# Swapping the two loop levels of the vector engine's gate multiply in a product-key expert layer

## The chip, the cores and the metric

The kernel runs on one core of a Trainium2 chip. The metric is the device time of one execution in microseconds, as the median over executions of the same program. Lower is better.

## The reference

Two transformer blocks are computed in fp32 on 256 tokens of width 1024. The part around the change is the expert layer of the first block: 16384 experts, each a row of `u` and a row of `v`, of which every token takes 16 for each of 8 heads.

```python
q = (xt @ w_q).reshape(BLOCK, PEER_HEADS, PEER_QDIM)
...
t1, i1 = lax.top_k(s1, PEER_TOPK)
t2, i2 = lax.top_k(s2, PEER_TOPK)
...
g = jax.nn.softmax(ts, axis=-1)
act = jax.nn.gelu(jnp.einsum('chkd,cd->chk', u[idx], xt))
coef = (g * act.astype(jnp.float32)).astype(xt.dtype)
return jnp.einsum('chk,chkd->cd', coef, v[idx])
```

## The kernel before

Every weight of the program comes as one stream of 128x128 fp32 tiles, eight to a slab (666 slabs). ScalarE copies each slab to a rounded part `whi` (L390), and VectorE or GpSimd subtracts that from the raw slab to make the remainder `wlo` (L407, in `split_lo`); in the expert layer every third slab goes to GpSimd. TensorE does three matmuls for each tile (`mm3`): high by high, high by low and low by high. The slab loads are issued on the SP queue, which waits for the remainder of the slab three places back.

The expert layer doesn't gather rows. It computes the products of all 128 groups of 128 experts with all tokens (the `u` phase, loop over `e`), applies gelu, and keeps the result in SBUF as two buffers, `act1` and `act2`, each of 64 key indices `i` by 256 tokens `t`, with the token index running fastest: the element (i, t) of a half lies at column 256 i + t. The gate of each (expert, token) pair is zero nearly everywhere. It is built by a product of one-hot matrices: for each group `g` of 8 tokens, VectorE writes the one-hot matrix `ohA` of the second key (L1838), the one-hot matrix `oh` of the first key (L1840) and its product with the three bf16 parts of the gate, `ohB` (L1845). TensorE then runs 24 matmuls of 64 columns into one PSUM bank (8 tokens by 64 key indices, the key index running fastest), and `multiply` (L1847 to L1851) multiplies the piece of the `act` buffer that belongs to these 8 tokens by that bank, in place. In half 0 the profile calls the one-hot buffers `act` too, because they lie in `act2`, which is free until then; in half 1 they have buffers of their own, `ohA`, `oh` and `ohB`.

There are 32 groups in each half. The steps are spread by hand over the tile stream: `coef_tiles` puts the 34 steps of half 0 among the `u` tiles of `e` from 64 to 111, and the 34 steps of half 1 among the `v` tiles of `e` from 0 to 60. A step `j` on VectorE is `multiply(half, j - 2)` and then `onehots(half, j)`. On TensorE, the step for group `g` waits for the multiply of group g - 4 (its PSUM bank is one of four) and for `ohB` of group `g`. In the `v` phase each finished chunk `act[e]` (256 contiguous columns) is split again, by ScalarE into `c` high (`c_hi`) and by VectorE into `c` low (L330), and then multiplied with the `v` tiles. All instructions of an engine run in the order in which the program gives them, so that the multiply stands in VectorE's queue among the slab remainders, the one-hot operations and the `c` remainders.

Of the kernel before, what the change touches and what calls it, by code (L numbers as in the profile page):

```python
# [15 lines left out]
ALU = mybir.AluOpType  # L16
# [9 lines left out]
NX = 256  # L26
# [37 lines left out]
TG, NCF = 8, 3  # L64
# [1599 lines left out]
def dve_peer(k, ring):  # L1664
    V, s, b, p, PS, vec = k.V, k.s, k.b, k.p, k.PS, k.nc.vector
# [179 lines left out]
        s["oh"].inc(vec.tensor_tensor(out, one, rows, ALU.mult))  # L1845

    def multiply(half, g):  # L1847
        v = p.halves[half][:, :].rearrange("p (i t) -> p i t", t=NX)[:, :, TG * g:TG * g + TG]
        V.wait_ge(s["cpe"], NG * half + g + 1)
        V.wait_ge(s["gelu"], HK * (half + 1))  # L1850
        s["coef"].inc(vec.tensor_tensor(v, PS[:, 4 + g % 4, :].rearrange("p (t i) -> p i t", t=TG), v, ALU.mult))  # L1851

    def coefs(half, j):
        if j > 1:
            multiply(half, j - 2)
        if j <= NG:
            onehots(half, j)
# [1345 lines left out]
```

## Time and profile before

| | |
|---|---|
| median of three executions | 2210.39 us |
| lowest and highest | 2207.11 and 2212.05 us |
| the profiled execution | 2212.05 us, its span 2210.7 us |
| TensorE busy in the span | 97% |
| VectorE busy in the span | 73% |
| ScalarE, GpSimd busy | 52%, 29% |
| mean granted TensorE clock | 0.992 |
| the 64 multiplies at L1851 | 43.7 us in all, starting from 557.4 to 955.6 us |

The span runs from the first to the last instruction; 1.35 us of the profiled execution's time lie outside it. Busy times of TensorE are of pipelined matmuls whose ends are modelled, so whether TensorE is held up is read from its waits and from the distance between the starts of its instructions.

### The profile page before, as it was taken

The numbers are of one execution on the slowest core, as the hardware profiler recorded it, in microseconds if no ns is written. First come the engines' busy times: TensorE is split into PE (matmuls) and PEld (weight loads), VectorE is DVE, ScalarE is ACT, GpSimd is POOL, SyncE is SP. The second block draws the span as 40 slices with busy tenths as digits, with TensorE's granted clock in tenths as the row PEclk, the third lists the DMA queues.
The fourth block names the chain that finished last, engine by engine and source line by source line (L and its number), as shares of the span: only waits on it lengthen the run. The fifth ranks groups of instructions, "written<-read, shape, count | busy, mean of one in ns | idle before, by whom it ended". The sixth has DMA issues, their size and how long they took to land.

```text
span 2210.7 us, 44628 instructions
## 1 busy us (share of the span) xinstructions
PE 2150.5 (97%) x18600; PEld 2113.3 (96%) x18600; DVE 1621.7 (73%) x2601; ACT 1160.2 (52%) x1980; POOL 630.7 (29%) x510
## 2 busy tenths in 40 slices
PE   8999999999999999999999999989999999999997
PEld 8898999999999999999999998979999999899997
DVE  7787767798987499965567647988655864788664
ACT  6776565454333444444465445756455544566443
POOL 7422244233222232333333004963001100113001
PEclk9999999999999999999999999999999999999999
DMA  5432455555445544455555554215554655544553
GB/s 169 156 129 96 156 167 177 177 184 175 163 153 159 177 155 162 159 177 182 184 171 188 184 191 134 68 48 162 191 191 141 195 188 193 177 139 152 192 192 114
DMA packets 101143, 357.35 MB, mean 162 GB/s; under 512 B 12048, under 2 KB 15440, under 8 KB 100816
## 3 DMA queue, kind: packets, MB, share of 16 engines
q1 hardware_dynamic: 100080, 352.35, 48.7%
q8 instruction: 148, 2.42, 0.4%
q10 hardware_dynamic: 864, 2.16, 0.3%
q14 instruction: 51, 0.42, 0.1%
HBM read 352.86 MB, written 1.05 MB: 160 GB/s over the span
## 4 chain that ended last, share of the span: by engine, by line
PE 82%; DVE 9%; POOL 3%; ACT 3%; issue 2%; DMA 1%; SPq 0%; POOLq 0%; ACTq 0%; DVEq 0%
PE PS L319 82%; POOL dgl L2975 2%; DVE wlo L407 2%; DVE H L2649 1%; DVE bn L2600 1%; DVE w L2714 1%; DMA raw<-stream 1%; DVE H L2647 1%; ACT whi L327 1%; DVE XC L1056 1%; ACT bsq L327 0%; DVE n L330 0%; DVE gate L1232 0%; POOL XC L1302 0%; DVE XR L1171 0%
## 5 line engine op out<-in xcount | busy, mean ns | idle before, releaser
L407 DVE TENSOR_TENSOR wlo<-raw,whi 128x1024 fp32r<-128x1024 f32 x546 | 686.6, 1260 | 216.5 <-ACT whi L327 215.7
L327 ACT ACTIVATE whi<-raw 128x1024 fp32r<-128x1024 f32 (+1 forms) x667 | 698.9, 1050 | 165.5 <-PE PS L319 101.5
L319 PE MATMUL PS<-bn,whi 128*128 128x256 f32 x3328 | 595.5, 281 | 16.4 <-ACT bn L327 4.9
L319 PEld LDWEIGHTS PS<-bn,whi 128*128 128x128 f32 x3328 | 509.8, 188 | 22.2 <-issue 12.0
L407 POOL TENSOR_TENSOR wlo<-raw,whi 128x1024 fp32r<-128x1024 f32 x119 | 324.2, 2725 | 695.5 <-ACT whi L327 695.4
L319 PE MATMUL PS<-n,whi 128*128 128x256 f32 (+1 forms) x2784 | 516.7, 287 | 5.3 <-DVE wlo L404 3.3
L319 PE MATMUL PS<-bn,wlo 128*128 128x256 f32 x1664 | 459.1, 280 | 0.0
L319 PEld LDWEIGHTS PS<-n,whi 128*128 128x128 f32 x2784 | 436.1, 192 | 9.5 <-issue 4.0
L319 PE MATMUL PS<-n,wlo 128*128 128x256 f32 (+1 forms) x1392 | 395.6, 284 | 0.0
L319 PE MATMUL PS<-c,whi 128*128 128x256 f32 x2048 | 372.3, 284 | 0.0
L319 PEld LDWEIGHTS PS<-c,whi 128*128 128x128 f32 x2048 | 318.9, 192 | 0.0
L319 PEld LDWEIGHTS PS<-bn,wlo 128*128 128x128 f32 x1664 | 313.0, 188 | 0.0
L319 PE MATMUL PS<-c,wlo 128*128 128x256 f32 x1024 | 289.5, 283 | 0.0
L319 PEld LDWEIGHTS PS<-n,wlo 128*128 128x128 f32 x1392 | 267.7, 192 | 0.0
L319 PE MATMUL PS<-hh,whi 128*128 128x256 f32 x1408 | 253.6, 283 | 0.0
L319 PEld LDWEIGHTS PS<-hh,whi 128*128 128x128 f32 x1408 | 219.6, 192 | 0.0
L319 PE MATMUL PS<-hh,wlo 128*128 128x256 f32 x704 | 199.2, 283 | 0.0
L319 PEld LDWEIGHTS PS<-c,wlo 128*128 128x128 f32 x1024 | 196.3, 192 | 0.0
L330 DVE TENSOR_TENSOR c<-act,c 128x256 fp32r<-128x256 f32 x128 | 81.2, 635 | 113.4 <-ACT c L327 113.4
L327 ACT ACTIVATE c<-act 128x256 fp32r<-128x256 f32 x128 | 53.5, 418 | 207.2 <-PE PS L319 207.2
L327 ACT ACTIVATE act<-PS 128x256 f32<-128x256 f32 x128 | 49.3, 385 | 210.6 <-PE PS L319 210.5
L1943 POOL TENSOR_TENSOR acc<-bsq 128x256 f32<-128x256 f32 x12 | 11.1, 922 | 468.5 <-ACT bsq L327 468.5
(351 smaller groups left out, 2995.1 us busy)
## 6 DMA issues: line engine op xcount, KB each, us to landing
raw<-stream SPq DMA_DIRECT2D x666, 512.0 KB, 3.3
abias<-c_alibi ACTq DMA_DIRECT2D x1, 1536.0 KB, 6.3
H<-xt SPq DMA_DIRECT2D x4, 256.0 KB, 6.2
out<-H SPq DMA_DIRECT2D x3, 256.0 KB, 2.4
mask<-c_mask SPq DMA_DIRECT2D x1, 272.0 KB, 6.5
K<-Vh SPq DMA_DIRECT2D x2, 136.0 KB, 4.6
K<-Vl SPq DMA_DIRECT2D x2, 136.0 KB, 5.1
out<-H ACTq DMA_DIRECT2D x2, 128.0 KB, 1.9
```

The source lines that it names most:

```text
L319: return self.nc.tensor.matmul(out, l, r, start=start, stop=stop, skip_group_check=True)
L327: return self.nc.scalar.activation(out, in_, func, **kw)
L330: return self.nc.vector.tensor_tensor(out, x, hi.bitcast(F32), ALU.subtract)
L407: k.s[q].inc(me.e.tensor_tensor(lo[:, :], raw[:, :], hi[:, :].bitcast(F32), ALU.subtract))
L1056: ins = vec.scalar_tensor_tensor(b.XC[:, m, :], b.XR[:, m, t:t + T], col("cw", t * NC + m), b.XC[:, m, :], ALU.mult, ALU.add)
L1943: s["acc"].inc(pool.tensor_tensor(k.acc, sq[:, 0, :] if c == 1 else k.acc, sq[:, c, :], ALU.add))
L2600: s["pre_lo"].inc(k.nc.vector.scalar_tensor_tensor(x[:, c, 1, :], k.X[c], pre_gain(k, pre, c), x[:, c, 0, :].bitcast(F32), ALU.mult, ALU.s ...
L2647: V.step(vec.tensor_tensor(k.X[c], k.X[c], z.rp, ALU.mult))
L2649: s["x_new"].inc(vec.tensor_tensor(k.X[c], k.X[c], z.F[:, c, :], ALU.add))
L2714: ins = vec.scalar_tensor_tensor(c.w[:, q, :], c.u[:, q, t:t + NX], z.wdw[:, j:j + 1], c.w[:, q, :], ALU.mult, ALU.add)
L2975: s["dgl"].inc(pool.tensor_tensor(c.dgl[:, i % NDG, :], k.ident, c.wl[:, j:j + 1].broadcast_to([128, 128]), ALU.mult))
```

## The change

One function is edited. The multiply reads and writes the same elements as before, with the two levels of its loop exchanged: the token index is now the outer one and the key index the inner one, in all three operands.

```diff
     def multiply(half, g):
-        v = p.halves[half][:, :].rearrange("p (i t) -> p i t", t=NX)[:, :, TG * g:TG * g + TG]
+        v = p.halves[half][:, :].rearrange("p (i t) -> p t i", t=NX)[:, TG * g:TG * g + TG, :]
         V.wait_ge(s["cpe"], NG * half + g + 1)
         V.wait_ge(s["gelu"], HK * (half + 1))
-        s["coef"].inc(vec.tensor_tensor(v, PS[:, 4 + g % 4, :].rearrange("p (t i) -> p i t", t=TG), v, ALU.mult))
+        s["coef"].inc(vec.tensor_tensor(v, PS[:, 4 + g % 4, :].rearrange("p (t i) -> p t i", t=TG), v, ALU.mult))
```

Before, the innermost 8 elements of a row are contiguous in SBUF, and 256 bytes apart in PSUM. After, all 512 elements are contiguous in PSUM, and the innermost 64 elements of a row are 1024 bytes apart in SBUF, for the operand read as for the one written. The number of instructions, their sizes, their order on the engine and their waits are the same.

## Rows read from the trace of the kernel before

**Rows 1.** The page: busy time, share and instructions; then the granted TensorE clock in 40 slices.

```profile
PE 2150.5 (97%) x18600; PEld 2113.3 (96%) x18600; DVE 1621.7 (73%) x2601; ACT 1160.2 (52%) x1980; POOL 630.7 (29%) x510
...
PEclk9999999999999999999999999999999999999999
```

**Rows 2.** By stretch: us, busy of PE, PEld, DVE, ACT, POOL; clock, DMA share, GB/s.

```profile
557.00:702.00 145.00, 145.00 (x1726) 143.71 (x1721) 133.97 (x151) 56.99 (x85) 36.79 (x14) 1.00 0.49 160
702.00:757.00 55.00, 55.00 (x478) 55.00 (x477) 16.88 (x18) 26.10 (x41) 14.41 (x6) 1.00 0.52 168
757.00:951.00 194.00, 193.43 (x2169) 191.56 (x2168) 177.88 (x224) 80.27 (x117) 61.03 (x20) 1.00 0.49 161
```

**Rows 3.** Who waited for whom, 550 to 960: total us, times, longest.

```profile
PE PS L319 <- DVE ohB L1845: 0.6, 2, 0.3
```

**Rows 4.** VectorE's waits in 557 to 702, then in 757 to 951.

```profile
DVE wlo L407 <- ACT whi L327: 8.9, 5, 3.3
...
DVE c L330 <- ACT c L327: 13.9, 21, 1.1
```

**Rows 5.** VectorE's groups by line and shape: total us, mean ns of one.

```profile
L1851 DVE TENSOR_TENSOR act<-PS,act 128x512 f32<-128x512 f32 x64 | 43.7, 683 | 0.0
...
L330 DVE TENSOR_TENSOR PT<-PS,PT 128x512 fp32r<-128x512 f32 x16 | 10.8, 676 | 0.8 <-ACT PT L327 0.4
...
L1171 DVE TENSOR_TENSOR_SCAN XR<-R,XC 128x272 f32<-128x272 f32 x8 | 9.7, 1230 | 0.0
...
L1670 DVE TENSOR_TENSOR H<-H,PS 128x256 f32<-128x256 f32 x8 | 3.3, 413 | 1.4 <-PE PS L319 1.4
```

**Rows 6.** VectorE's slab remainders within 557 to 702: total us, mean ns.

```profile
L407 DVE TENSOR_TENSOR wlo<-raw,whi 128x1024 fp32r<-128x1024 f32 x30 | 36.4, 1220 | 9.0 <-ACT whi L327 8.9
```

**Rows 7.** Timeline around 561 us: start, length; first VectorE, then GpSimd.

```profile
561.16 0.69 DVE L1851 TENSOR_TENSOR act<-PS,act 128x512 f32<-128x512 f32 x1
561.76 2.28 DVE L1838 TENSOR_TENSOR act<-iT,iota 128x1024 bf16<-128x1024 bf16 x1
...
567.15 0.68 DVE L1838 TENSOR_TENSOR act<-iT,iota 128x1024 bf16<-128x1024 bf16 x1
...
561.00 2.50 POOL L407 TENSOR_TENSOR wlo<-raw,whi 128x1024 fp32r<-128x1024 f32 x1 [7.81 <-ACT whi L327]
```

**Rows 8.** Half 0: VectorE's ohB, then TensorE's 24 matmuls, second and last group.

```profile
555.36 0.96 DVE L1845 TENSOR_TENSOR act<-act,gp 128x1536 bf16<-128x1536 bf16 x1
...
695.29 3.18 DVE L1845 TENSOR_TENSOR act<-act,gp 128x1536 bf16<-128x1536 bf16 x1
...
556.46 0.86 PE L319 MATMUL PS<-act 128*128 128x64 bf16 x24
...
701.99 0.87 PE L319 MATMUL PS<-act 128*128 128x64 bf16 x24
```

**Rows 9.** Half 1, timeline from 894 us: VectorE, GpSimd; then TensorE's critical groups.

```profile
894.79 0.43 DVE L330 TENSOR_TENSOR c<-act,c 128x256 fp32r<-128x256 f32 x1 [0.73 <-ACT c L327]
...
896.27 0.69 DVE L1851 TENSOR_TENSOR act<-PS,act 128x512 f32<-128x512 f32 x1
896.87 2.30 DVE L1838 TENSOR_TENSOR ohA<-iT,iota 128x1024 bf16<-128x1024 bf16 x1
...
899.66 0.96 DVE L1845 TENSOR_TENSOR ohB<-oh,gp 128x1536 bf16<-128x1536 bf16 x1
...
895.79 2.83 POOL L407 TENSOR_TENSOR wlo<-raw,whi 128x1024 fp32r<-128x1024 f32 x1 [6.13 <-ACT whi L327]
...
781.17 0.86 PE L319 MATMUL PS<-ohB,ohA 128*128 128x64 bf16 x24
...
900.77 0.86 PE L319 MATMUL PS<-ohB,ohA 128*128 128x64 bf16 x24 [0.29 <-DVE ohB L1845]
...
931.03 0.86 PE L319 MATMUL PS<-ohB,ohA 128*128 128x64 bf16 x24 [0.29 <-DVE ohB L1845]
```

**Rows 10.** VectorE around 684 us: the multiply of group 27.

```profile
684.12 0.68 DVE L1851 TENSOR_TENSOR act<-PS,act 128x512 f32<-128x512 f32 x1
```

## Prediction

> **What bounds the kernel now.** I read the page first. TensorE is busy for 97% of the span at a granted clock of 9 tenths or more throughout, VectorE for 73% [rows 1]. The page's average says little about the change, which touches 64 VectorE instructions between 557 and 956 us, so the second view is the busy time by stretch. Beside the two halves of the gate work TensorE has no hole to speak of (145.00 of 145 us, 193.43 of 194), and VectorE is at 134.0 of 145 us in half 0 and at 177.9 of 194 us in half 1, against 16.9 of 55 us in the gap between them [rows 2]. The reader is to see two engines that are nearly full at the same time, with TensorE the one that sets the pace.
>
> The third view is the waits. Over the whole stage TensorE waited for VectorE twice, 0.6 us in all, both times for `ohB` [rows 3]. VectorE waited 8.9 us in half 0 and 13.9 us in half 1, always for ScalarE, whose pieces follow TensorE's progress [rows 4]. So a longer or a shorter VectorE instruction changes the end only by what its slack does not take up, and a shorter one can return at most those 0.6 us.
>
> The fourth view is the groups by line. L1851 takes 683 ns for 512 elements of a row, 43.7 us in all, with no wait in front of it [rows 5].
>
> **The change, step by step.** Nothing is removed, added or moved: 64 instructions with the same elements, waits and place in the queue. What can change is the time of one.
>
> *Now.* Two rows of the same kind, one PSUM and one SBUF operand, give the rate. 256 elements take 413 ns (`H<-H,PS`), 512 take 676 ns (`PT<-PS,PT`, contiguous everywhere) [rows 5]. That is (676 - 413) / 256 = 1.03 ns for each element and about 150 ns fixed. The multiply takes 683 ns, 7 ns above the contiguous row. It already runs at one element in 1.03 to 1.04 ns, although it reads PSUM in steps of 256 bytes. This bounds the gain: making PSUM contiguous returns at most 7 ns x 64 = 0.4 us of VectorE time.
>
> *After, lower bound.* If the step of 1024 bytes in SBUF is as free as the step of 256 bytes in PSUM is now, one multiply takes 676 to 683 ns, and nothing moves.
>
> *After, upper bound.* No row of before has VectorE read or write SBUF with a large innermost step, so the price is unknown upward. Two rows stand for it. If each element takes the time of two, the multiply costs what 1024 elements cost, 1220 ns as for the slab remainder [rows 6], which is 0.537 us more. The slowest rate of a two-operand row here is the scan's, (1230 - 150) / 272 = 3.97 ns for each element [rows 5], which would make the multiply 512 x 3.97 + 150 = 2180 ns, 1.50 us more. I take the lower bound. The only large step that the trace shows at all is free, and the row it belongs to is this instruction's own.
>
> A page speaks against that. The Trainium skill, "SBUF — State Buffer", section "Door 1: The DMA port swizzle (why `[64,N]` ≈ `[32,N]`)", says that accesses that go to a new 16-byte line each time pay a penalty in SBUF, so that fp32 data may be stepped only within four elements for free. It gives no figure for VectorE. It also names 8-byte lines for PSUM, with a slowdown that it states for matmuls; the trace does not bear such a slowdown out for VectorE's read, since 256-byte steps cost 7 ns in 683. By that rule the time is that of the first rival below; by the rows it is unchanged. Against it stands "VectorE: DVE Perf Modes", section "Mode 1× (REGULAR) — the baseline", by which odd strides run at one element a cycle in this mode.
>
> *Where the time would go.* TensorE's work per group of tokens is fixed: the groups start at 556.46 and, 30 groups later, at 701.99 us, 4.85 us apart [rows 8]. Behind the multiply in VectorE's queue stand `ohA`, `oh` and `ohB` of the group two further on, then slab remainders and, in half 1, `c` remainders. TensorE waits for `ohB` first. The multiply itself is wanted late: that of group 27 ends at 684.12 + 0.68 = 684.80 us [rows 10], and the group that needs its bank starts at 701.99 us [rows 8], 17 us later. So at unchanged price the sum is 2212.05 us for the profiled execution + 0 - up to 0.4 us. The profiled execution is the slowest of three, 1.66 us above their median; the sum against the median is 2210.4 us.
>
> **Rival 1: SBUF steps cost double.** Place: `ohB` comes late. Price: 0.537 us x 64 = 34.4 us of VectorE time. In half 0, 30 multiplies lie before the last `ohB`, 16.1 us. Of these 8.9 us fall into VectorE's waits [rows 4]. The last `ohB` ends at 698.47 us and is wanted at 701.99 us, a margin of 3.5 us [rows 8]. That leaves 3.7 us of delay to TensorE. In half 1, 16.1 us stand against 13.9 us of waits, but the margin vanishes at every fifth group: there VectorE waits for ScalarE at 894.79 us, does one multiply at 896.27, and ends `ohB` at 900.62 us, with TensorE already waiting [rows 9]. Six groups look like this, each with a margin of 0.15 us or less, the first at 781.17 and the last at 931.03 us [rows 9], and slack ahead of the wait does not help them: 6 x 0.537 = 3.2 us. Together 6.9 us. Walking all 64 groups in the same way (lateness grows by 0.537 us at each multiply, shrinks by each wait but not below TensorE's own lateness, and passes to TensorE when it exceeds the margin of that `ohB`) gives 10.9 us, the upper figure, because early margins are small: 0.14 us for the group at 556.46 us [rows 8].
>
> Something works against it. `ohA` at 561.76 us takes 2.28 us where an undisturbed one takes 0.68, and ends just after a GpSimd remainder of 561.00 to 563.50 us, while the multiply that started at 561.16, within that remainder, took its usual 0.69 us [rows 7]. In the critical group above it is the same: `ohA` is held until about GpSimd's end (895.79 + 2.83 = 898.62 us), so that 0.537 us more in the multiply would first come out of a block of 1.6 us [rows 9]. GpSimd is busy 36.8 of 145 us [rows 2], so a quarter or more of the extra is free. The Trainium skill, "SBUF — State Buffer", section "Who interferes with whom", states the rule (one SBUF operand does not contend, two do, for a whole instruction), and the trace agrees in these rows. With everything absorbed the rival costs 0. Its range is 0 to 10.9 us, 2212.05 to 2223.0 us, and its likeliest figure about 4 us, 2216 us. It decides (more than 0.2%, 4.4 us) from about 0.4 us more for one multiply with nothing absorbed: the same walk at 0.4 us gives 4.3 us.
>
> **Rival 2: SBUF steps cost as much as the scan or more.** Place and end are the same, 1.50 us x 60 = 90 us, less 22.8 us of waits [rows 4], less a quarter hidden under GpSimd: between 45 and 67 us late, 2257 to 2279 us. VectorE would then be the bound of both halves. For it speaks only that read and write are both stepped; against it, no plain two-operand row in the profile runs at such a rate.
>
> **Rival 3: faster.** PSUM read in order could relieve more than VectorE's 7 ns, say TensorE's writes to the other banks. But TensorE's tiles in this stage keep their distance, and only the 0.6 us of waits [rows 3] can be returned: 2211.4 us, no measurable gain. Only a reason outside the profile makes this more than 4.4 us.
>
> **How the numbers follow.** Unchanged price: 0.62, almost all of it within 0.2%, which is about what three executions from 2207.11 to 2212.05 us can tell from no change; 0.02 of it on each side for the scatter. Rival 1: 0.26, half within 0.2% and half slower. Rival 2: 0.08, slower. Rival 3 as a real gain: 0.04. That makes faster 0.06, same 0.71, slower 0.23. The prediction is that of the unchanged price, 2210.4 us. The range reaches down to 2206 us, 1 us under the lowest run, and up to 2223 us, the upper figure of rival 1; rival 2 is left out. The likeliest case's own range is 2206 to 2214 us.
>
> **What would show it right or wrong.** L1851 at 676 to 690 ns, x64, confirms the price; 1220 ns is rival 1; 2 us or more is rival 2. VectorE's busy time in the two halves should stay at 134 and 178 us, TensorE's wait for `ohB` at about 0.6 us, and the groups of TensorE 4.85 us apart in half 0. The prediction is wrong if a step over SBUF costs VectorE more than about 0.4 us for 512 elements and GpSimd's blocks don't take it up, or if the longer multiply shifts the queue so that more two-operand instructions meet GpSimd's remainders than do now.

## The result and the profile after

The changed kernel took 2229.61 us (median of five, 2225.6 to 2231.03) against 2212.05 us for the one before, timed beside it (2207.11 to 2215.8). The ratio is 1.0076, with a 95% interval of 1.0056 to 1.0095: slower by 12 to 21 us, and outside the range that was forecast, 2206 to 2223 us.

The groups by line of the changed kernel, VectorE, 540 to 980 us (total us, mean ns of one):

```profile
L407 DVE TENSOR_TENSOR wlo<-raw,whi 128x1024 fp32r<-128x1024 f32 x86 | 117.7, 1372 | 29.3 <-ACT whi L327 29.3
L1851 DVE TENSOR_TENSOR act<-PS,act 128x512 f32<-128x512 f32 x64 | 85.0, 1329 | 0.0
```

The multiply went from 683 [rows 5] to 1329 ns, 41.3 us more in all. Among VectorE's rows it is the only one whose own work takes longer; the others that grew, grew where a GpSimd instruction held them, as the runs without GpSimd's share show below. The page of the profile still shows TensorE at 97% and the same clock slices; the change is visible only by stretch. Here is the same view as [rows 2], with the halves reaching to their new last group:

```profile
557.00:709.00 152.00, 146.46 (x1723) 143.87 (x1722) 149.94 (x149) 56.97 (x84) 38.40 (x14) 1.00 0.45 148
770.00:963.00 193.00, 186.25 (x2095) 183.62 (x2095) 187.66 (x215) 77.82 (x112) 52.47 (x19) 1.00 0.46 151
```

VectorE is now at 149.9 of 152 us and 187.7 of 193 us, and TensorE has holes of 5.5 and 6.8 us where it had 0 and 0.6. The waits say who caused them (TensorE, 550 to 980 us, then VectorE's in the second half; in half 0 VectorE now waits for nobody, 8.9 us before [rows 4]):

```profile
PE PS L319 <- DVE ohB L1845: 6.6, 8, 1.4
PE PS L319 <- DVE act L1845: 5.3, 8, 1.4
```

```profile
DVE c L330 <- ACT c L327: 3.1, 6, 1.1
```

Both rows of TensorE are waits for `ohB`, which the profile calls `act` in half 0: 11.9 us against 0.6 [rows 3]. The same shows in the starts of TensorE's groups of 24 matmuls. First and last of each half:

```profile
551.43 0.87 PE L319 MATMUL PS<-act 128*128 128x64 bf16 x24
...
708.79 0.86 PE L319 MATMUL PS<-act 128*128 128x64 bf16 x24 [0.72 <-DVE act L1845]
...
770.05 0.87 PE L319 MATMUL PS<-ohB,ohA 128*128 128x64 bf16 x24
...
962.60 0.87 PE L319 MATMUL PS<-ohB,ohA 128*128 128x64 bf16 x24
```

The kernel before started the same groups at 551.70, 701.99, 763.26 and 948.84 us. Half 0 grew from 150.3 to 157.4 us, half 1 from 185.6 to 192.6 us: 7.1 + 7.0 = 14.0 us, unrounded. The spans differ by 2225.4 - 2210.7 = 14.7 us. So what the two profiled executions differ by lies almost wholly in these two stretches. TensorE's waits grew by 11.3 us only. They are counted from modelled ends, so the starts are the safer measure.

### The profile page after: what moved, and what is told of

It is laid out like the page before. It is cut to its first block, busy times and chain, and to the rows that moved or that the text cites. A ratio compares the mean times of both kernels' runs of the same rounds, so it can differ in the third digit from the quotient of the medians.

```text
span 2225.4 us, 44628 instructions
## 1 busy us (share of the span) xinstructions
PE 2151.7 (97%) x18600; PEld 2112.7 (95%) x18600; DVE 1660.4 (75%) x2601; ACT 1161.9 (52%) x1980; POOL 626.5 (28%) x510
## 3 DMA queue, kind: packets, MB, share of 16 engines
HBM read 352.86 MB, written 1.05 MB: 159 GB/s over the span
## 4 chain that ended last, share of the span: by engine, by line
PE 69%; DVE 20%; POOL 4%; ACT 3%; issue 3%; DMA 1%; SPq 0%; POOLq 0%; DVEq 0%; ACTq 0%
PE PS L319 69%; DVE wlo L407 5%; DVE act L1851 3%; POOL dgl L2975 2%; DVE act L1845 2%; DVE act L1838 1%; DVE c L330 1%; DMA raw<-stream 1%; DVE ohB L1845 1%; DVE ohA L1838 1%; ACT whi L327 1%; DVE bn L2600 1%; DVE H L2649 1%; DVE w L2714 1%; DVE H L2647 1%
## 5 line engine op out<-in xcount | busy, mean ns | idle before, releaser
L407 DVE TENSOR_TENSOR wlo<-raw,whi 128x1024 fp32r<-128x1024 f32 x546 | 697.0, 1280 | 205.6 <-ACT whi L327 205.1
L319 PE MATMUL PS<-bn,whi 128*128 128x256 f32 x3328 | 596.1, 281 | 17.1 <-ACT bn L327 4.9
```

Source lines behind the costliest of these rows:

```text
L319: return self.nc.tensor.matmul(out, l, r, start=start, stop=stop, skip_group_check=True)
L407: k.s[q].inc(me.e.tensor_tensor(lo[:, :], raw[:, :], hi[:, :].bitcast(F32), ALU.subtract))
```

## The experiments

Theory: each SBUF element in a line of its own costs VectorE extra time, that time makes `ohB` late, and TensorE waits. This is theory 1 below. Rivals: the cost hangs on very wide jumps (theory 2), or on working in place (theory 3); or the stepped accesses slow other engines.

**The price by itself.** A program that only multiplies, 512 elements a row, four of each kind, each after the end of the one before. Its core:

```python
tt = lambda o, a, b: vec.tensor_tensor(o, a, b, ALU.mult)
it = lambda x: x.rearrange("p (i t) -> p i t", t=256)[:, :, 8:16]
ti = lambda x: x.rearrange("p (i t) -> p t i", t=256)[:, 8:16, :]
by = lambda x, s: x[:, 0:512 * s:s]
...
tt(it(X), pit, it(X))                           # the order of before
tt(ti(X), pti, ti(X)); tt(ti(Y), pti, ti(X))    # the order of after; into another buffer
tt(wti, pti, ti(X)); tt(ti(Y), pti, uti)        # only the read stepped; only the write
tt(W, PS, by(X, s)); tt(by(Y, s), PS, U)        # steps of s = 2, 3, 4, 8, 16, 32 elements
```

> A program that computes nothing of the reference: VectorE multiplies alone, 512 elements a row, four of each kind, one at a time, with PSUM or SBUF operands at different steps, and a few ScalarE copies. Both theories expect about 676 ns with everything contiguous, 680 ns for the order of before and 1275 to 1330 ns for the order of after, in place. 
Some of its rows (timeline: start, length). The first three are the order of after in another buffer, the read alone stepped, the write alone stepped; then runs of 4, reads at steps of 2, 3, 4 and 8 elements, and a write at 32. The two rows of ScalarE are a contiguous copy and one that reads at 256-element steps.

```profile
50.92 1.24 DVE L30 TENSOR_TENSOR Y<-PS,X 128x512 f32<-128x512 f32 x1
...
56.01 1.01 DVE L30 TENSOR_TENSOR W<-PS,X 128x512 f32<-128x512 f32 x1
...
60.18 1.02 DVE L30 TENSOR_TENSOR Y<-PS,U 128x512 f32<-128x512 f32 x1
...
68.02 0.69 DVE L30 TENSOR_TENSOR X<-PS,X 128x512 f32<-128x512 f32 x1
...
70.92 0.69 DVE L30 TENSOR_TENSOR W<-PS,X 128x512 f32<-128x512 f32 x1
...
73.96 0.82 DVE L30 TENSOR_TENSOR W<-PS,X 128x512 f32<-128x512 f32 x1
...
77.62 1.05 DVE L30 TENSOR_TENSOR W<-PS,X 128x512 f32<-128x512 f32 x1
...
81.97 1.06 DVE L30 TENSOR_TENSOR W<-PS,X 128x512 f32<-128x512 f32 x1
...
114.03 1.02 DVE L30 TENSOR_TENSOR Y<-PS,U 128x512 f32<-128x512 f32 x1
...
128.25 0.63 ACT L88 ACTIVATE W<-U 128x512 f32<-128x512 f32 x1
...
130.23 1.06 ACT L90 ACTIVATE W<-X 128x512 f32<-128x512 f32 x1
```

The kinds with one PSUM operand, in microseconds for 512 elements (the four of a kind agree within 0.01):

| VectorE, one PSUM operand | read stepped | written stepped | both |
|---|---|---|---|
| contiguous, PSUM in order | | | 0.69 |
| the order of before (8 contiguous, PSUM steps of 256 bytes) | | | 0.69 |
| runs of 2 or of 4 tokens innermost | | | 0.69 |
| 2 elements (8 bytes) | 0.69 | 0.69 | |
| 3 elements (12 bytes) | 0.83 | 0.83 | |
| 4 elements (16 bytes) | 1.05 | 1.06 | |
| 8 elements | 1.06 | 1.08 | |
| 16 and 32 elements | 1.01 | 1.02 | |
| 256 elements, 64 to a run (the order of after) | 1.01 | 1.02 | 1.24 |

A part of the cost shows at 12 bytes, all of it at 16, and from there it is nearly flat for one stepped side. Theory 2, wide jumps, is out for a single side. So is theory 3: in place and into another buffer both take 1.24 us. At 12 bytes half of the elements share a 16-byte line with a neighbour, and the price, 0.14 us of 0.36, lies a little below halfway. Theory 1 has the line right and the size wrong for one side: a stepped read or write alone costs 0.32 us more, and only both together 0.55. At this step they neither hide behind each other nor add up in full. With both sides stepped the width does count: at 16 bytes both together took 1.06 us and at 128 bytes 1.12 to 1.14, against 1.24 at 1024 bytes. Those two rows had their other input in SBUF and not in PSUM, so step and memory are not told apart.

The rule that I weighed and set aside is that of the Trainium skill, "SBUF — State Buffer", section "Door 1: The DMA port swizzle (why `[64,N]` ≈ `[32,N]`)": two accesses to each 16-byte line are needed for full bandwidth. The trace agrees: 8-byte steps and runs of 2 are free, 16-byte steps are not. At 12 bytes, which that section's free range of four fp32 elements would seem to cover, the trace has 0.83 us against 0.69.

**The same in the kernel.** The exchange undone halfway: four contiguous tokens innermost.

```diff
-        v = p.halves[half][:, :].rearrange("p (i t) -> p i t", t=NX)[:, :, TG * g:TG * g + TG]
+        v = p.halves[half][:, :].rearrange("p (i t) -> p i t", t=NX)[:, :, TG * g:TG * g + TG].rearrange("p i (h l) -> p h i l", l=4)
...
-        ... PS[:, 4 + g % 4, :].rearrange("p (t i) -> p i t", t=TG), v, ALU.mult))
+        ... PS[:, 4 + g % 4, :].rearrange("p (h l i) -> p h i l", l=4, i=HK), v, ALU.mult))
```

> The multiply with tokens in two runs of 4 (outer), the key index, and 4 contiguous tokens (16 bytes) innermost. Theory 1 (16-byte lines): the multiply takes 680 to 700 ns and the kernel the time of before, 0.998 to 1.002. Theory 2 (wide jumps): 64 x 2 jumps of 1024 bytes instead of 64, and 128 jumps cost at least a fourth of the extra 646 ns, about 840 ns, and by the slack walk less than 1 us in the end, 1.000.

Ratio to before 1.0001 (0.9992 to 1.0010), with the multiply unchanged:

```profile
L1851 DVE TENSOR_TENSOR act<-PS,act 128x512 f32<-128x512 f32 x64 | 43.7, 682 | 0.0
```

It visits twice as many places 1024 bytes apart as the order of before and costs nothing. That fits theory 1: what costs is a line that gives one element only.

**Why 1.33 us in the kernel and 1.24 alone.** The multiply in the changed order beside one other engine at a time, then beside three.

```python
start(by_act, by_pe, by_dma)       # ScalarE copy 128x6144, 24 matmuls of 512 columns, a 2 MB load
for _ in range(10):
    go(vec.tensor_tensor(ti(X), pti, ti(X), ALU.mult))
```

> A program that computes nothing of the reference: the multiply in the changed order alone, then with ScalarE copying, TensorE multiplying, a DMA writing to SBUF, GpSimd subtracting, and the first three together; at the end the order of before with the three together. Alone it took 1.24 us, in the changed kernel 1.33 us. If other traffic at SBUF slows a stepped access, one of the companions brings 1.24 to about 1.33 us and all three at least as much, while the order of before stays at 0.68 to 0.69 us. If the 0.09 us come from something else (where the buffer lies, say), all stay at 1.24 us.

One row beside ScalarE, one beside ScalarE, TensorE and the load, and one of the order of before beside all three:

```profile
42.90 1.27 DVE L77 TENSOR_TENSOR X<-PS,X 128x512 f32<-128x512 f32 x1
...
79.58 1.33 DVE L93 TENSOR_TENSOR X<-PS,X 128x512 f32<-128x512 f32 x1
...
90.84 0.69 DVE L97 TENSOR_TENSOR X<-PS,X 128x512 f32<-128x512 f32 x1
```

The multiply took 1.24 us alone, beside ScalarE's copy 1.27 to 1.29, TensorE 1.28 to 1.29, GpSimd 1.25 to 1.27, the load 1.24. Beside the three, 1.30 to 1.35 while ScalarE and TensorE run, and 1.24 again once they have ended. The order of before stays at 0.69 throughout. So the last 0.09 us come from what ScalarE and TensorE do meanwhile, and only the stepped order feels it. ScalarE's copy touches nothing but SBUF, so there the two meet at SBUF; TensorE also writes PSUM, and for it the place is not shown.

**One half alone.**

```diff
+        v = p.halves[half][:, :].rearrange("p (i t) -> p t i" if half == 0 else "p (i t) -> p i t", t=NX)
+        v = v[:, TG * g:TG * g + TG, :] if half == 0 else v[:, :, TG * g:TG * g + TG]
```

(and the PSUM operand likewise)

> The exchanged order in half 0 alone, the order of before in half 1. In the changed kernel the 31 steps between the first and the last group of TensorE grew by 7.1 us in half 0 and by 7.0 us in half 1. If VectorE's lateness is the whole cause, this run has the 7 us of half 0 and none of half 1: 1.003 (1.002 to 1.0045), with 32 multiplies at about 1330 ns and 32 at 683. If the two halves interact (the lateness of one is carried into the other), it lies at 1.005 or more, or at 1.001 or less.

Ratio 1.0032 (1.0020 to 1.0044), 7.1 us. TensorE waited 5.4 us in half 0 and, as before, 0.6 us in half 1. From first to last group half 0 grew to 157.4 us as in the changed kernel and half 1 stayed at 185.6. The halves are independent:

```profile
PE PS L319 <- DVE act L1845: 5.4, 8, 1.4
PE PS L319 <- DVE ohB L1845: 0.6, 2, 0.3
```

**The same lateness without the step.**

```diff
+        bank = PS[:, 4 + g % 4, 0:448]
+        step(vec.tensor_copy(bank, bank))
+        V.wait_step()
```

> The order of before, and ahead of each multiply a VectorE copy of 448 columns of its PSUM bank onto itself, which touches no SBUF and adds about 0.65 us to VectorE's queue, the same as the exchanged order does. If the whole loss is VectorE's time in the queue, this kernel loses as much as the changed one: 14 to 20 us, 1.006 to 1.009. If a part of the loss comes from the stepped accesses themselves (other engines slowed at SBUF), it loses clearly less, 1.004 or below.

Ratio 1.0065 (1.0051 to 1.0079); TensorE waited for `ohB` as in the changed kernel, 11.9 us in all:

```profile
PE PS L319 <- DVE act L1845: 6.1, 10, 1.5
PE PS L319 <- DVE ohB L1845: 5.8, 7, 1.3
```

From its start to that of the multiply behind it the copy takes 0.66 us, where the exchange added 0.63. So an instruction that touches no SBUF and takes about the same time from VectorE's queue costs the same within the intervals (the two halves grew by 13.3 us together, against 14.0). Within them, nothing is left that the stepped accesses would have to cost elsewhere.

**A smaller and a larger dose.** The same edit with 128 columns, then twice with 512.

> The order of before, with a copy of 128 columns of PSUM onto itself ahead of each multiply: 0.33 us more in VectorE's queue, as much as a step on one side only (read or written) costs. The lateness theory has a threshold: the walk over the groups gives 0 to 3.2 us, 1.000 to 1.0015. If every added microsecond reached the end in proportion (14.7 us for 0.65 us), it would be 7.5 us, 1.0034.

> The order of before, with two copies of 512 columns of PSUM ahead of each multiply: 1.44 us more each. The lateness theory has VectorE full from the first groups on, so that nearly all that is above the slack arrives: 60 x 1.44 = 86 us less 22.8 us of waits is 63 us, 1.028 (1.024 to 1.031). In proportion to the 0.65 us it would be 33 us, 1.015. If GpSimd's blocks absorbed a quarter, 45 us or less, 1.020.

The small dose gave 1.0028 (1.0019 to 1.0038), 6.2 us; the large one 1.0269 (1.0249 to 1.0289), 59.5 us.

```profile
L1852 DVE COPY PS<-PS 128x128 f32<-128x128 f32 x64 | 18.7, 292 | 0.0
```

That row is the small dose's copy: 0.29 us and some 0.04 us for the wait behind it. The large dose came out near the queue sum with nothing absorbed (63 us), and not in proportion (33 us). The small one missed: the walk over the groups allowed 3.2 us at most. It had assumed that GpSimd's blocks, the time by which GpSimd's instructions hold up VectorE's, stay on the instructions on which they lay. Counted from first to last group, as time above the undisturbed length, they grew from 25.1 to 26.8 us in half 0 and from 27.8 to 31.6 us in half 1. Here the longer queue met more of GpSimd's instructions, which the prediction's last sentence had named as a way to be wrong.

**GpSimd's blocks taken away.** The changed order, with VectorE doing the remainders of slabs 154 to 278 itself.

```diff
-    return (10 <= s <= 18 and s % 2 == 0) or (21 <= s <= 345 and s % 3 == 0) or (417 <= s <= 431 and s % 3 == 0)
+    return (10 <= s <= 18 and s % 2 == 0) or (21 <= s <= 345 and s % 3 == 0 and not 154 <= s < 279) or (417 <= s <= 431 and s % 3 == 0)
```

> The changed order, and VectorE does all slab remainders of the expert layer's two halves itself (slabs 154 to 278), GpSimd none. It adds 42 remainders of 1.14 us to VectorE's queue, 48 us, and takes away the blocks by GpSimd, 55 us in all. The theory that VectorE's time in the queue is what counts: VectorE gains 7 us and TensorE's loss falls from 14 to about 9 us, 1.004 to 1.006. Rival: the blocks lie mostly where VectorE had time, and 48 us more work make it worse, 1.009 or more.

Ratio to before 0.9996 (0.9987 to 1.0005). The slow multiply is still there, and the loss is gone; TensorE waited for nobody. VectorE's rows, 540 to 980 us:

```profile
L407 DVE TENSOR_TENSOR wlo<-raw,whi 128x1024 fp32r<-128x1024 f32 x131 | 158.6, 1219 | 23.1 <-ACT whi L327 23.0
L1851 DVE TENSOR_TENSOR act<-PS,act 128x512 f32<-128x512 f32 x64 | 84.8, 1325 | 0.0
...
L1838 DVE TENSOR_TENSOR act<-iT,iota 128x1024 bf16<-128x1024 bf16 x32 | 22.0, 687 | 0.0
```

`ohA` of half 0 is back at 687 ns (996 before and 973 in the changed kernel, both between 540 and 980 us), because no GpSimd instruction holds it. That was better than either side of my expectation. A net 7 us less in VectorE's queue was to leave 9 us of the loss; it left none. Most of the difference is a miscount of mine, since not all the remainders that VectorE took over lie within the halves. These are its remainders from first to last group, half 0 of the changed kernel and of this one, then half 1 of both:

```profile
L407 DVE TENSOR_TENSOR wlo<-raw,whi 128x1024 fp32r<-128x1024 f32 x30 | 47.2, 1584 | 0.0
L407 DVE TENSOR_TENSOR wlo<-raw,whi 128x1024 fp32r<-128x1024 f32 x45 | 53.8, 1219 | 0.0
...
L407 DVE TENSOR_TENSOR wlo<-raw,whi 128x1024 fp32r<-128x1024 f32 x37 | 47.2, 1277 | 0.0
L407 DVE TENSOR_TENSOR wlo<-raw,whi 128x1024 fp32r<-128x1024 f32 x55 | 67.0, 1219 | 0.0
```

VectorE took over 15 and 18, 33 and not 42. In half 0 they cost 15 x 1.14 = 17.1 us and 24.2 us of blocks are gone, which is 7.1 us net, the whole loss of that half (150.3 us again). In half 1 they cost 20.5 us against 25.7 us of blocks, 5.2 us net; VectorE's waits and its lead at the last `ohB` gave up 1.9 us more. The half fell by 8.2 us, to 184.4, so that about 1 us of it is not accounted for.

**The reverse and the counterpart.** GpSimd takes every second slab there (`s % (2 if 154 <= s < 279 else 3) == 0`) with the changed order; and the order of before without GpSimd's share.

> The changed order, and GpSimd takes every second slab of the two halves instead of every third. VectorE has about 21 remainders less to do, 24 us, and about 21 blocks more, which cost 1.6 us each in half 0 of the changed kernel (22.3 us over 14) and 1.5 in half 1, 32 us. By VectorE's time in the queue that is 8 us more, and the ratio to before rises from 1.007 to 1.009 to 1.012. Rival: GpSimd's work is help on balance and the loss of the changed kernel shrinks, 1.005 or less.

> The order of before, and VectorE does all slab remainders of the two halves (slabs 154 to 278) itself. With the changed order this move took back the whole loss and half 1 became 1.2 us shorter than in the kernel before. The theory that VectorE's time in the queue counts only through ohB: TensorE's waits of 0.6 us vanish and half 1 is again about 184.4 us instead of 185.6, in all 0 to 2 us less, 0.999 to 1.000, not to be told from no change. Rival: VectorE's 40 us of freed time shortens more than TensorE's waits show, 0.997 or less.

With every second slab the ratio rose to 1.0130 (1.0112 to 1.0148), 28.8 us. GpSimd's help is a loss for VectorE here, by a little more than I expected (1.009 to 1.012). Its waits:

```profile
PE PS L319 <- DVE ohB L1845: 15.2, 8, 3.0
PE PS L319 <- DVE act L1845: 8.4, 8, 1.7
PE PS L319 <- DVE wlo L407: 0.9, 1, 0.9
```

The order of before without GpSimd's share gave 0.9996 (0.9984 to 1.0007). TensorE's 0.6 us of waits are gone, and half 1 is 1.2 us shorter from first to last group (761.92 to 946.30 us, 184.4 us), twice what the waits showed; the time is not to be told from the kernel before. No kernel tried was measurably faster than that one.

## Why the prediction was wrong

**The reading of the stage was right.** TensorE sets the pace, VectorE is nearly full, `ohB` is the first thing to be late, the multiply itself is wanted 17 us later, and a shorter multiply could return next to nothing. The rows of after bear out the first four: all new waits are for `ohB`. The last fits the order of before without GpSimd's share, only that there up to 1.2 us could come back and not the 0.6 that the prediction had.

**The step that failed is the price: "I take the lower bound".** It was put at 676 to 683 ns and is 1329 ns. The argument was that the one large step in the trace, 256 bytes in PSUM, is free. That is true, and measured again in the stride program, but it says nothing of SBUF, where steps of 16 bytes and more cost 0.32 us and up. The prediction had no row with such a step in SBUF, so its rows could not decide, and it filled the gap with the row of another memory. The rule in "Door 1" of the Trainium skill, which spoke of SBUF, pointed the right way. Against it I had set the Trainium skill, "VectorE: DVE Perf Modes", section "Mode 1× (REGULAR) — the baseline", by which odd strides all work in the mode of one result a cycle. They work, but the traces do not bear out that they keep the pace: 512 elements took 1.01 to 1.08 us where contiguous ones took 0.69.

**Rival 1 is what happened, with two terms too small.** Its price was 0.537 us more; it is 0.646, of which 0.55 is the step itself and the rest traffic of ScalarE and TensorE. And its likeliest end, 4 us, rested on "a quarter or more of the extra is free" under GpSimd's instructions. No run bears that out. What VectorE lost to blocks in half 0 is its time above the undisturbed length (rows of the changed kernel, 557 to 709 us):

```profile
L407 DVE TENSOR_TENSOR wlo<-raw,whi 128x1024 fp32r<-128x1024 f32 x29 | 43.8, 1521 | 0.0
...
L1845 DVE TENSOR_TENSOR act<-act,gp 128x1536 bf16<-128x1536 bf16 x30 | 32.9, 1096 | 1.0
L1838 DVE TENSOR_TENSOR act<-iT,iota 128x1024 bf16<-128x1024 bf16 x30 | 29.8, 992 | 0.0
```

29 x (1.52 - 1.22) + 30 x (1.10 - 0.96) + 30 x (0.99 - 0.68) = 8.7 + 4.2 + 9.3 = 22 us. The kernel before has these rows from its first to its last group of half 0:

```profile
L1845 DVE TENSOR_TENSOR act<-act,gp 128x1536 bf16<-128x1536 bf16 x31 | 40.5, 1306 | 1.1
L407 DVE TENSOR_TENSOR wlo<-raw,whi 128x1024 fp32r<-128x1024 f32 x31 | 39.8, 1291 | 9.0 <-ACT whi L327 8.9
L1838 DVE TENSOR_TENSOR act<-iT,iota 128x1024 bf16<-128x1024 bf16 x31 | 31.2, 1006 | 0.0
```

By the same sum that is 10.8 + 2.2 + 10.0 us, and 2.1 us on `oh`, 25 us in all; the changed kernel has 24 us between its own first and last group. So 1 us of blocks was absorbed and not a quarter of 19. They moved from `ohB` and `ohA` to the slab remainders and stayed as long. My reading is that a longer multiply hides a block only where the two still meet, and that the queue shifts so that GpSimd meets something else. The large dose, 1.46 us a group, did absorb 6 of its 44 us in half 0 by the same count (25.1 to 18.8), also less than a quarter.

**With the right price and no absorption my simple sum fits half 0.** An instruction of VectorE starts a little before the one ahead of it has ended, so what one takes from the queue is read from start to start. In the changed kernel (timeline, half 1):

```profile
903.14 1.33 DVE L1851 TENSOR_TENSOR act<-PS,act 128x512 f32<-128x512 f32 x1
904.38 0.69 DVE L1838 TENSOR_TENSOR ohA<-iT,iota 128x1024 bf16<-128x1024 bf16 x1
...
906.78 1.22 DVE L407 TENSOR_TENSOR wlo<-raw,whi 128x1024 fp32r<-128x1024 f32 x1
907.91 0.42 DVE L330 TENSOR_TENSOR c<-act,c 128x256 fp32r<-128x256 f32 x1
```

A remainder takes about 1.14 us so, and the multiply 1.24 us (mean over the 64), where it took 0.60: 0.63 more, unrounded. 30 x 0.63 = 19.0 us, less 8.9 us of waits that vanished, less 3.4 us of margin at the last `ohB` (3.5 before, 0.1 after) is 6.7 us; the groups show 7.1. For half 1 the same sum is 19.0 less 10.8 us of waits (13.9 to 3.1) less 0.6 of margin, 7.6 us; measured 7.0.

**The upper end of the range** was that rival's walk at 0.537 us, 10.9 us. At 0.646 the walk gives 16.8 us and the groups show 14.0, but at 0.33 us it gives 3.2 where the groups show 5.5 and the times 6.2. So the threshold that I named, 0.4 us, was too high: the small dose alone was already slower by 0.28% (0.19 to 0.38). The price, 0.646 in place of 0.537 us, put the result 6.6 us above the range.

**What stays open.** Why a stepped read and a stepped write together cost 0.55 us here and no more than one of them at 16-byte steps, why steps of 16 to 32 bytes cost 0.04 us more than wider ones, and the last 1 us that half 1 gained when GpSimd's share was taken away. In that kernel `ohB` was 0.4 us or more ahead in every group, though VectorE had next to no idle time; that evenness counts beside the sum is my reading, and no run tested it by itself.

## What to carry to other kernels

Keep at least two fp32 elements of each 16-byte line together in every SBUF operand of VectorE, read or written: lone elements cost 0.32 us or more in 0.69 here; ScalarE paid too at the one step tried. In PSUM VectorE's reads in steps of 256 bytes were free, so where one side has to be stepped, let it be PSUM. Where no row of a profile shows an access pattern, another memory's row is no bound for it: take a rule of the Trainium skill on that memory, here that of "Door 1" on SBUF's 16-byte lines, as a rival at full weight, or leave the range open to it. Before spending VectorE's slack, look at what GpSimd blocks: here its "help" with a third of the remainders cost VectorE 1.6 us a piece (22 us over 14 in half 0) to save 1.14 us, and taking it back paid for a multiply twice as slow. It paid only there: with the order of before, where VectorE had slack, the same move gave nothing measurable.

## What the runs showed of the hardware that I had not expected

- ScalarE pays as VectorE does: a 512-element copy took 0.63 us contiguous, 1.06 us with the read stepped by 1024 bytes, and 1.06 us with the write stepped.
- Of the two orders of the multiply only the stepped one felt ScalarE and TensorE: 1.24 us alone, up to 1.35 us beside both, while the multiply with runs of 8 stayed at 0.69 us beside the same traffic. A load to SBUF by itself changed nothing (1.24 us).
- With both inputs in SBUF and one of them, and the result, at 16-byte steps, the multiply took 1.06 us, no more than with a stepped write alone. At 32 elements it took 1.12 to 1.14 us.
